# Two-layer encoder trunk on one core: the first products in single k tiles, the last tile in two column halves

## The reference

```python
def sqrelu_mlp(h, w_up, w_down):
    u = jax.nn.relu(h @ w_up)
    return (u * u) @ w_down

for layer in range(DEPTH):                       # DEPTH = 2
    h = rmsnorm(x, norm_mix_w[layer])
    y = hybrid_mixer(h, ...) if layer % 2 == 0 else swa_sink_attention(h, ...)
    x = x + y
    h = rmsnorm(x, norm_mlp_w[layer])
    x = x + sqrelu_mlp(h, mlp_w_up[layer], mlp_w_down[layer])
return rmsnorm(x, final_norm_w)
```

## Time and profile before

| What | Value |
|---|---|
| Median of three runs | 2016.05 us (2015.67 to 2016.38) |
| Profiled execution, its own time | 2016.07 us |
| Its span, first to last instruction | 2014.3 us |
| TensorE busy | 2003.6 us |
| VectorE busy | 1438.7 us |
| ScalarE busy | 1019.9 us |
| Mean rate of the DMA engines | 190 GB/s |

### The profile page before, as it was taken

One profiled execution on the slowest core, in us unless ns is written; L12 is line 12 of the kernel. 1 busy time (PEld: TensorE's weight loads), 2 busy tenths in 40 slices (PEclk: granted clock), 3 DMA queues, 4 the chain that ended last, 5 costly groups with the idle time before them and its releaser, 6 DMA issues.

```text
span 2014.3 us, 24679 instructions
## 1 busy us (share of the span) xinstructions
PE 2003.6 (99%) x9187; PEld 1655.2 (82%) x9187; DVE 1438.7 (71%) x1975; ACT 1019.9 (51%) x1345; POOL 45.2 (2%) x55
## 2 busy tenths in 40 slices
PE   9999999999999999999999999999999999999998
PEld 7888888888888888888888877888888888888886
DVE  6777778987558657846888777978548756854875
ACT  6665665455345435434545555555435434544554
POOL 1110110000000000000000000000000000000000
PEclk9999999999999999999999999999999999999999
DMA  8556556556566656565656535566565656565563
GB/s 303 186 170 213 169 167 209 189 187 210 189 188 197 199 188 189 197 197 176 202 187 200 174 129 167 186 193 202 192 191 190 202 188 187 187 208 188 188 202 112
DMA packets 191437, 382.50 MB, mean 190 GB/s; under 512 B 6264, under 2 KB 7040, under 8 KB 191232
## 3 DMA queue, kind: packets, MB, share of 16 engines
q1 hardware_dynamic: 190112, 377.58, 57.7%
q0 software_dynamic: 1216, 3.88, 0.6%
q10 hardware_dynamic: 32, 0.01, 0.0%
HBM read 379.34 MB, written 2.10 MB: 189 GB/s over the span
## 4 chain that ended last, share of the span: by engine, by line
PE 95%; DVE 3%; ACT 2%; issue 0%; ACTq 0%
PE acc L1127 31%; PE acc L1129 30%; PE acc L1128 30%; ACT w_hi L579 1%; DVE w_lo L788 1%; PE bank L1158 0%; PE bank L1237 0%; PE bank L1261 0%; PE bank L1247 0%; DVE area L868 0%; PE acc L1278 0%; ACT L648 0%; ACT L654 0%; DVE turn L835 0%; PE bank L1191 0%
## 5 line engine op out<-in xcount | busy, mean ns | idle before, releaser
L788 DVE TENSOR_TENSOR w_lo<-raw,w_hi 128x1024 fp32r<-128x1024 f32 x712 | 865.5, 1225 | 520.2 <-ACT w_hi L579 517.4
L579 ACT ACTIVATE w_hi<-raw 128x1024 fp32r<-128x1024 f32 x712 | 748.1, 1059 | 809.0 <-PE acc L1129 805.6
L1127 PE MATMUL acc<-w_hi,a_hi 128*128 128x512 f32 x1568 | 614.6, 392 | 0.0
L1129 PE MATMUL acc<-w_hi,a_lo 128*128 128x512 f32 x1568 | 610.4, 389 | 0.0
L1128 PE MATMUL acc<-w_lo,a_hi 128*128 128x512 f32 x1568 | 610.3, 389 | 0.0
L1127 PE MATMUL acc<-w_hi,b_hi 128*128 128x512 f32 x1264 | 492.4, 390 | 0.0
L1129 PE MATMUL acc<-w_hi,b_lo 128*128 128x512 f32 x1264 | 491.8, 389 | 0.0
L1128 PE MATMUL acc<-w_lo,b_hi 128*128 128x512 f32 x1264 | 491.8, 389 | 0.0
L1127 PEld LDWEIGHTS acc<-w_hi,a_hi 128*128 128x128 f32 x1568 | 294.4, 188 | 62.6 <-issue 1.8
L1129 PEld LDWEIGHTS acc<-w_hi,a_lo 128*128 128x128 f32 x1568 | 294.3, 188 | 61.7
L1128 PEld LDWEIGHTS acc<-w_lo,a_hi 128*128 128x128 f32 x1568 | 294.4, 188 | 60.2
(11 more groups left out here) (171 smaller groups left out, 587.1 us busy)
## 6 DMA issues: line engine op xcount, KB each, us to landing
raw<-in_mlp_w_up SPq DMA_DIRECT2D x128, 1024.0 KB, 5.5
raw<-in_mlp_w_down SPq DMA_DIRECT2D x128, 1024.0 KB, 5.1
raw<-in_hyb_w_in SPq DMA_DIRECT2D x44, 1024.0 KB, 5.2
raw<-in_attn_w_qkv SPq DMA_DIRECT2D x20, 1024.0 KB, 5.1
raw<-in_hyb_w_out SPq DMA_DIRECT2D x16, 1024.0 KB, 5.2
raw<-in_attn_w_out SPq DMA_DIRECT2D x16, 1024.0 KB, 5.1
raw<-in_hyb_w_in SPq DMA_DIRECT2D x8, 512.0 KB, 9.9
out_y<-x SPq DMA_DIRECT2D x4, 512.0 KB, 3.0
```

What stands on the lines that cost most here:

```text
L579: nc.scalar.activation(w_hi[:, h % RING], raw[:, h // 2, 2 * (h % 2):2 * (h % 2) + 2, :], ACT.Copy).then_inc(hi_ready, 1)
L788: nc.vector.tensor_tensor(w_lo[:, h % RING], raw[:, h // 2, 2 * (h % 2):2 * (h % 2) + 2, :], w_hi[:, h % RING].bitcast(F32), ALU.subtract) ...
L1127: nc.tensor.matmul(a, xh, wh, start=first, stop=False)
L1129: ins = nc.tensor.matmul(a, xl, wh, start=False, stop=last)
```

## The change

The diff does four things.

1. **First loads on two queues.** ScalarE's queue issues the identity, the norm weights, and the first two k tiles of weights as two copies of 256 KB (`raw_first[0]`, `raw_second`). SP starts with the two pieces of x.
2. **First half by single k tiles.** TensorE turns the first 256 columns of x one k tile at a time into two banks. ScalarE and VectorE go through `first_half`: round k tile 0 of x, round k tile 0 of the weights (512 columns), then the same for k tile 1. TensorE goes through `first_products`: hi by hi for both token tiles, then the transposes of the next 256 columns of x, then hi by lo, then lo by hi; then k tile 1. The zeros are now products of 128 columns, five and two, and the last group is gone.
3. **Last half of the second token tile in two column halves.** `last_half` runs the six products of 512 columns as twelve of 256: first the left 256 columns in `acc`, then the right 256 in another bank (`bank[:, 0]`), each with a signal of its own. VectorE adds the left half, adds what `acc` holds of the right half, and then the other bank; ScalarE squares in two parts. The sums of the first three column blocks are prepared ahead, and the root takes the last partial sum as its input and the rest as its bias.
4. **Stores of 512 columns.** For the second token tile SP issues four stores, each when its own columns are scaled.

```diff
 # SP: start and end
-            sp.dma_start(ident[:, :], t["ident"]).then_inc(ident_loaded, 16)
+                load_x(0, NB // 2, x_first)
+                load_x(NB // 2, NB, x_loaded[0])
                 for q in range(UNITS):
                     w = view(q, 0)
-                    if q == 0:
-                        load_x(0, NB // 2, x_first)
-                    elif q > 1:
+                    if q > 1:
                         load_x(q * NB, (q + 1) * NB, x_loaded[q])
-                    sp.dma_start(raw[:, q, 0:2], w[:, 0:2]).then_inc(raw_first[q], 16)
-                    if q == 0:
-                        load_x(NB // 2, NB, x_loaded[0])
+                    if q > 0:
+                        sp.dma_start(raw[:, q, 0:2], w[:, 0:2]).then_inc(raw_first[q], 16)
...
+            for j, scaled, n in ((1, y_dve, 3), (0, y_act, 3), (3, y_dve, 4), (2, y_act, 4)):
+                sp.wait_ge(scaled, n)
+                sp.dma_start(y_dram[:, 1, j * NB:(j + 1) * NB], x[:, 1, j * NB:(j + 1) * NB]).then_inc(stored, 16)
 # ScalarE: start
+            act.dma_start(ident[:, :], t["ident"]).then_inc(ident_loaded, 16)
             act.dma_start(vec_rows[0:KT, 0, :], ...).then_inc(norm0_loaded, 16)
+            act.dma_start(raw[:, 0, 0:1], w0[:, 0:1]).then_inc(raw_first[0], 16)
+            act.dma_start(raw[:, 0, 1:2], w0[:, 1:2]).then_inc(raw_second, 16)
...
+            def first_half():
+                for e in range(2):
+                    act.wait_ge((x_turned, turned)[e], 1)
+                    nc.scalar.activation(a_hi[:, e, :], bank[:, 2 * e, 0:SEQ], ACT.Copy,
+                                         scale=vec(e)).then_inc((x_hi, turned_hi)[e], 1)
+                    act.wait_ge((raw_first[0], raw_second)[e], 16)
+                    nc.scalar.activation(w_hi[:, 0, e, :], raw[:, 0, e, :],
+                                         ACT.Copy).then_inc((hi_first, hi_ready)[e], 1)
 # ScalarE: end
+                act.wait_ge(summed, SUMMED_FIRST + n)
+                nc.scalar.activation(rms[:, 4, tt:tt + 1], last_sum[:, 0:1], ACT.Sqrt, scale=1.0 / D_MODEL,
+                                     bias=ms[:, 4, tt:tt + 1]).then_inc(rms_ready, 1)
 # VectorE: end, second tile
+                    nc.vector.tensor_tensor(xs[:, left], xs[:, left], done[:, left], ALU.add).then_inc(evac_dve, 1)
+                    link(nc.vector.tensor_tensor(xs[:, right], xs[:, right], done[:, right], ALU.add))
+                    dve.wait_ge(tile_done, tt + 2)
+                    nc.vector.tensor_tensor(xs[:, right], xs[:, right], bank[:, 0, left], ALU.add).then_inc(evac_dve, 1)
 # TensorE: first half
+            def first_products():
+                for e in range(2):
+                    wh, wl = w_hi[:, 0, e, :], w_lo[:, 0, e, :]
+                    pe.wait_ge((x_hi, turned_hi)[e], 1)
+                    pe.wait_ge((hi_first, hi_ready)[e], 1)
+                    for tt in range(TT):
+                        a, xh = acc[:, 0, tt, :], a_hi[:, e, tt * P:(tt + 1) * P]
+                        nc.tensor.matmul(a, xh, wh, start=e == 0, stop=False)
+                    if e == 0:
+                        pe.wait_ge(x_loaded[0], 16)
+                        turn_block(x[:, :, 0:NB], 0, (1,))
+                    pe.wait_ge((lo_first, lo_ready)[e], 1)
...
 # TensorE: last half of the second tile
+            def last_half(b, tt):
+                k = HALVES - 1
+                for c in range(2):
+                    a = bank[:, 0, 0:NB // 2] if c else acc[:, b % 2, tt, 0:NB // 2]
+                    for e in range(2):
...
+                        nc.tensor.matmul(a, xh, wh, start=c == 1 and e == 0, stop=False)
+                        nc.tensor.matmul(a, xh, wl, start=False, stop=False)
+                        ins = nc.tensor.matmul(a, xl, wh, start=False, stop=e == 1)
+                    ins.then_inc(tile_done, 1)
 # TensorE: zeros and first transposes
-                    ins = nc.tensor.matmul(acc[:, 1, 1, 0:SEQ], junk[:, 0:P], junk[:, 0:SEQ], start=True, stop=True)
+                    ins = nc.tensor.matmul(acc[:, 1, 1, 0:P], junk[:, 0:P], junk[:, 0:P], start=True, stop=True)
-            zeros(3)
+            zeros(5)
...
-            turn_block(x[:, :, 0:NB], 0, (0,))
+            for e in range(2):
+                for tt in range(TT):
+                    ins = nc.tensor.transpose(bank[:, 2 * e, tt * P:(tt + 1) * P], x[:, tt, e * P:(e + 1) * P],
+                                              ident[:, :])
+                ins.then_inc((x_turned, turned)[e], 1)
             zeros(2)
-            pe.wait_ge(x_loaded[0], 16)
-            turn_block(x[:, :, 0:NB], 0, (1,))
-            zeros(3)
```

More of the change, by code:

```diff
@@ L148 @@
 X_TURN_AT = {0: 1, 1: 2, 3: 3}
-ZEROS_GROUPS = 3
+ZEROS_GROUPS = 2
 N_EVAC_ACT = total(BY_ACT, TT)
@@ L163 @@
 N_SUMS = total({"res", "fin"}, TT)
+SUMMED_FIRST = N_SUMS[NBLK - 1] + TT * COLS
 class Slot:
@@ L493, in _ @@
             half = D_MODEL // 2
[L494 to L501, removed]
+            for m in range(2):
+                sp.wait_ge(y_act, m + 1)
+                sp.wait_ge(y_dve, m + 1)
+                sp.dma_start(y_dram[:, 0, m * half:(m + 1) * half],
+                             x[:, 0, m * half:(m + 1) * half]).then_inc(stored, 16)
+            for j, scaled, n in ((1, y_dve, 3), (0, y_act, 3), (3, y_dve, 4), (2, y_act, 4)):
+                sp.wait_ge(scaled, n)
+                sp.dma_start(y_dram[:, 1, j * NB:(j + 1) * NB], x[:, 1, j * NB:(j + 1) * NB]).then_inc(stored, 16)
+            sp.wait_ge(stored, 16 * 6)
         @block.gpsimd
@@ L1094, in _ @@
             last = slice((COLS - 1) * NB, COLS * NB)
+            dve.wait_ge(summed, SUMMED_FIRST)
+            link(nc.vector.tensor_reduce(ms[:, 4, :], sums[:, 4, :, 0:COLS - 1], AX_X, ALU.add))
+            nc.vector.tensor_scalar(ms[:, 4, :], ms[:, 4, :], 1.0 / D_MODEL, EPS,
+                                    ALU.mult, ALU.add).then_inc(ms_ready, 1)
             for tt in range(TT):
@@ L1097, in _ @@
                 xs = x[:, tt, last]
+                done = acc[:, (NBLK - 1) % 2, tt, :]
                 dve.wait_ge(tile_done, tt + 1)
[L1099 to L1102, removed]
-                                        ALU.mult, ALU.add).then_inc(ms_ready, 1)
+                if tt < TT - 1:
+                    nc.vector.tensor_tensor(xs, xs, done, ALU.add).then_inc(evac_dve, 1)
+                else:
+                    left, right = slice(0, NB // 2), slice(NB // 2, NB)
+                    nc.vector.tensor_tensor(xs[:, left], xs[:, left], done[:, left], ALU.add).then_inc(evac_dve, 1)
+                    link(nc.vector.tensor_tensor(xs[:, right], xs[:, right], done[:, right], ALU.add))
+                    dve.wait_ge(tile_done, tt + 2)
+                    nc.vector.tensor_tensor(xs[:, right], xs[:, right], bank[:, 0, left], ALU.add).then_inc(evac_dve, 1)
+                    dve.wait_ge(ms_ready, 5)
+                    dve.wait_ge(summed, SUMMED_FIRST + tt + 1)
+                    m = ms[:, 4, tt:tt + 1]
+                    nc.vector.scalar_tensor_tensor(m, sums[:, 4, tt, COLS - 1:COLS], 1.0 / D_MODEL, m,
+                                                   ALU.mult, ALU.add).then_inc(ms_ready, 1)
                 dve.wait_ge(rms_ready, 5 + tt)
@@ L1140, in last_products @@
                             pe.wait_ge(lo_ready, slot.halves(k + 1))
+                        if tt == TT - 1 and k == HALVES - 1:
+                            last_half(b, tt)
+                            break
                         for e in range(2):
@@ L1303, in body @@
                 for k in range(HALVES):
-                    if b == 0:
+                    if b == 0 and k > 0:
                         pe.wait_ge(turned_out, k + 1)
```

66 lines of the change are left out of this document (51 added, 15 removed).

## The result

| | before | changed |
|---|---|---|
| Median | 2016.05 us | 2030.79 us (2030.06 to 2032.34, 4 runs) |
| Ratio, 95% interval | | 1.0074 [1.0062, 1.0086] |
| Span of the profiled execution | 2014.3 us | 2028.7 us |
| Copies of instructions (queue q8) | 49 | 67 |

A forecast was written before the change was run, and what follows sets the result against it. TensorE, busy 99% of the span, was taken to bound the kernel, with only its two ends changed. 2016.07 - 0.8 (start) - 0.85 (tail) = 2014.4 us, range 2012.9 to 2016.3, no measurable change.

The forecast's parts named there:

- The change touches only its two ends: Whole kernel: only the start and last stores' delay change; the product stream, TensorE busy 99% of the span, is not shortened.
- if the span changes anywhere between 30 and 2005 us: Middle of the kernel: one of the signs listed as showing the prediction wrong.
- with its 256 KB landed by 5.1: Start: first k tile of weights landed by 5.1, ready near 5.8, first products 3.1 us sooner than 8.96.
- interleaving eats the start: Start, rival at 15%: x's second quarter or second k tile lands a microsecond later, start gains 0; 2015.2 us.
- the clock stays low: Start, rival at 8%: more rest keeps TensorE at 1.2 GHz; 2018.5 us if low to the second half's end.
- The slack of 0.4 at x's third part: Start: that copy landed 0.4 us before its transposes at 15.43, limiting the gain; with 0.4 earlier landing, 0.8.
- Rests of some 0.5 us only: Start: the argument against a clock that stays low, that TensorE would rest only some 0.5 us.
- the 8% rival: Start, 8%: the same rival as "the clock stays low", 2018.5 us.
- The gate at x's third part: Start: TensorE, 2.0 us ahead by itself, waits for this copy; transposes at 14.6, gain held to 0.8 us.
- The start's gain: Start: 0.4 slack plus 0.4 earlier landing, 0.8 us gained, between 0.4 and 1.1.
- The end: Tail: column halves, prepared sums and earlier stores gain 0.89, taken as 0.85 us; bounds 0.9 and a loss of 0.15.
- ends 2.7 us after it starts: Tail: four stores of 256 KB, 0.69 us each at 381 GB/s; the transfer ends 2.7 us after it starts.

The follow-up runs named there:

- e1: The changed kernel with one more product of zeros at the start, four more TensorE instructions ahead of the first loop; 2017.92 us, ratio 1.0008.
- e2: The kernel before with two products of zeros instead of three at the start, four TensorE instructions fewer ahead of the first loop; 2029.72 us, ratio 1.0066.
- e10: The kernel before with 240 long-satisfied semaphore waits added to TensorE's stream ahead of the first loop; 2024.43 us, ratio 1.0042.
- e4: e1 with the first two k tiles of weights issued by SP, each behind its 256 columns of x, instead of by ScalarE; 2015.42 us, ratio 0.9996.
- e4_again: The same kernel as e4, run once more; 2014.85 us, ratio 0.9993.
- e9: The kernel before with 200 long-satisfied semaphore waits added to TensorE's stream ahead of the first loop; 2018.34 us, ratio 1.0009.
- e5: The kernel before with 80 long-satisfied semaphore waits added to TensorE's stream ahead of the first loop; 2018.28 us, ratio 1.0009.

## Why the prediction was wrong

**The step that failed first is one that it made in half a sentence**: "The change touches only its two ends". The stream of products between 30 and 2005 us was put at no change, without a reason. (The 1.8 us around the span did stay: 2030.49 less 2028.7.) I had priced every added and removed instruction by what it does and none by where it puts the code behind it. Three instructions fewer ahead of the loop cost 12.0 us (4.0 and 4.3 of rest at the loop's two returns and the clock behind them), 7 times what both ends were to bring. The prediction's own test ("if the span changes anywhere between 30 and 2005 us") named the place. e1 and e2 show it in both directions, e10 shows the price.

**The landing of the first k tile** ("with its 256 KB landed by 5.1") is the second. It came at 7.75. The total rate was little better with two queues: from 1.5 us to that landing the engines were 85% busy at 268 GB/s, in the kernel before 83% at 253 (the row below answers to 0.92 at 275 there). And ScalarE's copy had to share them with SP's copies of x and of the later weights, all issued in 0.76 to 3.4. I had walked it as though it went alone.

```profile
5.00:8.00 3.00, 1.58 (x8) 1.28 (x6) 0.48 (x1) 0.70 (x2) 0.00 (x0) 1.00 0.97 330
```

Of the rivals, "interleaving eats the start" named this mechanism, for x's second quarter or the second k tile and with a gain of 0 left over, and "the clock stays low" named what followed from it, at 2018.5. Together they are what e1 measured without the fetches: 2017.92. The rule that the prediction weighed there (the Trainium skill, "DMA: Bandwidth & Descriptors", Issuing engines are not separate DMA queues) was borne out in that the total hardly rose. It doesn't say which copy loses: here it was the one on the second queue, 6.1 us from issue to landing, and 3.7 and 3.9 in its place on SP's queue in e4 and e4_again. The slack of 0.4 at x's third part, on which the forecast rested, had nothing to say on the first copy.

**Rest and clock.** "Rests of some 0.5 us only" became one of 2.0 to 2.2, and the passes shortened at about 14.0 instead of 7.4. This is what the 8% rival described. That the rest kept the clock low is argued, not shown: e4_again had no such rest and its passes shortened only at about 10.8. The next transposes, which mark the first half's end, came at 14.34, not 9.8; the prediction had put its limit at 11.

**What held at the start.** The table load moved to 2.64 and ended at 3.92, hidden as said; the copies followed one another on ScalarE's queue at 0.46 to 0.48 (said: 0.48). The first 256 columns of x landed at 4.11, not 3.7. Zeros and transposes released ScalarE at 5.42 rather than 4.6, as the transposes waited for the norm weights until 4.43. The gate at x's third part is real once TensorE is early enough: in e4's trace this copy lands at 14.43 and its transposes start at 14.47 (said: 14.6). The start's gain with the weights on one queue is 0.2 to 0.8 us (the medians of e4 and e4_again below the kernel before, less the end's 0.46), against 0.8 forecast.

**The end** was right in mechanism and mis-sized in two terms. Twelve products at 0.12 (said: 0.115), VectorE last with three adds of 0.42 (said: 0.42), the third one 0.11 after the last product's recorded end (said: 0.25). The root takes 0.29 instead of 0.20 with its scale and bias, so the scaling gained 0.57, not 0.66, and the first store 0.78 to 0.80, not 0.89. The larger miss is the transfer, "ends 2.7 us after it starts". Windows of the changed kernel's last stores:

```profile
2024.75:2025.50 0.75, 0.00 (x0) 0.00 (x0) 0.00 (x0) 0.07 (x1) 0.00 (x0) 0.50 0.88 330
2025.50:2026.25 0.75, 0.00 (x0) 0.00 (x0) 0.00 (x0) 0.00 (x0) 0.00 (x0) 0.50 1.05 385
2026.25:2027.00 0.75, 0.00 (x0) 0.00 (x0) 0.00 (x0) 0.00 (x0) 0.00 (x0) 0.50 1.03 377
2027.00:2027.75 0.75, 0.00 (x0) 0.00 (x0) 0.00 (x0) 0.00 (x0) 0.00 (x0) 0.50 0.84 306
```

Against 381 GB/s over 2.75 us in the earlier trace rows it is now 350 over 3.0, and the last landing follows the first issue by 4.29 us instead of 3.95. So of 0.80 some 0.46 are left. That four stores of 256 KB move slower than two of 512 KB at the same size in all is measured; whether it is their shorter rows or their issue was not tried.

## What to carry to other kernels

- In a kernel with hardware loops on an engine that never rests, count that engine's instructions ahead of each loop before and after any edit. A change far away in time can move a loop's head over a block boundary; here 12.9 of the 14.7 us came back with one added product of zeros, and an edit's worth should be measured with the loop's place held fixed.
- A copy put on a second queue to be early competes with everything that the first queue has already issued. If the order of landing matters and the engines are busy, put it in its order on one queue.
- When a difference appears where the change isn't, read the queue of instruction copies and the rests by "issue" before looking for a cause in the data flow.

## What the runs showed that I had not expected

- TensorE's instructions come in copies of 16 KB, 256 instructions. A loop of 1614 instructions that spans 7 blocks runs its later passes with no copy; one that spans 8 is fetched in every pass (18 copies more over its second and third pass).
- A return into a block that is gone takes 3.3 to 5.0 us on the sequencer. The products queued ahead hide some 3.8 of it (e9: branches of 4.45 and 4.38 leave rests of 0.7 and 0.6; e5: one of 4.98 leaves 1.2). A second block needed at once leaves rests of 3.9 to 4.3 (changed, e2); 14 instructions in between leave 2.6 to 2.8, and 54 leave only the first fetch's excess, 0.4 to 1.2. Eight blocks were never held in these runs; whether one place is kept for fetching ahead or the memory ends there is open.
- After rests of 4.0 to 4.3 us the clock fell to its lower level for some 3.4 us in the changed kernel, and in e2 for as long after the first return and for about 6 after the second; in e10 it fell after one of 2.6 and not after one of 2.8. Rests of 0.7 and 1.2 had no such cost.
- One kernel can see its clock rise at different times at the start: 4.9 us in e4's trace, about 10.8 in e4_again's.
- Waits that are satisfied cost TensorE nothing that shows: 150 of them, 2016.06 against 2016.10 for the kernel before on the same chip.
